# Last rows of four wide output products by token halves, with their norms and the next stage's first tiles, and squares added on VectorE

## The reference

```
for i in (0, 1):
    x  = x  + 0.5 * g1 * swiglu(modulate(rms(x),  sh1, sc1), pre_wi[i], pre_wo[i])    # D_FF = 2816
    xc = xc + 0.5 * g1c * swiglu(modulate(rms(xc), ...), pre_wi[i], pre_wo[i])
    o, oc = mixer(modulate(rms(x), sh2, sc2), modulate(rms(xc), ...))   # i=0 differential, i=1 window attention
    x = x + g2 * o ;  xc = xc + cg2 * oc            # xc only for i=0
    x = ffn_step(x, ..., post_wi[i], post_wo[i]) ;  xc likewise only for i=0
rms(x) = x * rsqrt(mean(x*x, over the 1024) + 1e-6)
modulate(h, shift, scale) = h * (1 + scale) + shift
```

## Time and profile before

| | |
|---|---|
| Median of 3 runs | 3052.09 us (3051.44 to 3053.5) |
| Span of the profiled execution | 3059.4 us |
| TensorE busy | 2886.5 us (94% of the span) |
| Weight loads busy | 2378.0 us |
| VectorE busy | 1669.1 us (55%) |
| ScalarE busy | 1225.2 us (40%) |
| GpSimd busy | 251.8 us (8%) |
| Mean granted clock of TensorE | 0.972 of full speed |
| Chain that ended last | PE 85%, DVE 9%, ACT 2%, DMA 2%, issue 1% |

### The profile page before, as it was taken

One profiled execution on the slowest core, in us unless ns is written; L12 is line 12 of the kernel. 1 busy time (PEld: TensorE's weight loads), 2 busy tenths in 40 slices (PEclk: granted clock), 3 DMA queues, 4 the chain that ended last, 5 costly groups with the idle time before them and its releaser, 6 DMA issues.

```text
span 3059.4 us, 46813 instructions
## 1 busy us (share of the span) xinstructions
PE 2886.5 (94%) x16044; PEld 2378.0 (78%) x16044; DVE 1669.1 (55%) x2800; ACT 1225.2 (40%) x1979; POOL 251.8 (8%) x163
## 2 busy tenths in 40 slices
PE   7999989997899999999988889998799899999999
PEld 4777866753678887788866379996799899888888
DVE  3333337756433333433337555577579777677765
ACT  4322223345232222322223544456445455455554
POOL 2000003200010000100003000000048200000000
PEclk9999999999899999999999989999999999999999
DMA  6444221262152222222231535552256555567754
GB/s 263 170 166 168 99 90 65 80 220 104 35 186 96 96 100 93 85 98 97 98 103 62 181 130 192 186 192 90 104 186 206 168 177 172 190 242 241 242 202 144
DMA packets 144831, 444.88 MB, mean 145 GB/s; under 512 B 16088, under 2 KB 44888, under 8 KB 144224
## 3 DMA queue, kind: packets, MB, share of 16 engines
q1 hardware_dynamic: 112896, 409.51, 38.9%
q10 hardware_dynamic: 31840, 34.13, 3.2%
HBM read 428.37 MB, written 15.20 MB: 145 GB/s over the span
## 4 chain that ended last, share of the span: by engine, by line
PE 85%; DVE 9%; ACT 2%; DMA 2%; issue 1%; SPq 1%; POOL 0%; ACTq 0%; DVEq 0%
PE bank L1565 21%; PE bank L1566 20%; PE bank L1567 20%; PE bank L1979 11%; PE bank L1581 2%; PE bank L1951 2%; PE bank L1804 1%; PE bank L1845 1%; DMA raw<-w_stream_dram 1%; PE bank L1588 1%; DVE cand L1364 1%; PE bank L1816 1%; DVE stage_rs L1037 1%; PE bank L1658 1%; PE bank L1836 1%
## 5 line engine op out<-in xcount | busy, mean ns | idle before, releaser
L1565 PE MATMUL bank<-H,w_hi 128*128 128x256 f32 (+1 forms) x3232 | 1097.4, 340 | 54.8 <-DVE H L1028 47.1
L995 DVE TENSOR_TENSOR w_lo<-raw,w_hi 128x1024 fp32r<-128x1024 f32 x584 | 714.7, 1225 | 700.9 <-ACT w_hi L568 696.0
L1566 PE MATMUL bank<-H,w_hi 128*128 128x256 f32 (+1 forms) x3232 | 1068.6, 331 | 0.0
L1567 PE MATMUL bank<-H,w_lo 128*128 128x256 f32 (+1 forms) x3232 | 1068.4, 331 | 0.0
L568 ACT ACTIVATE w_hi<-raw 128x1024 fp32r<-128x1024 f32 x628 | 660.0, 1052 | 250.9 <-PE bank L1567 208.3
L1565 PEld LDWEIGHTS bank<-H,w_hi 128*128 128x128 f32 x3232 | 623.8, 193 | 147.7 <-issue 83.0
L1566 PEld LDWEIGHTS bank<-H,w_hi 128*128 128x128 f32 x3232 | 624.2, 193 | 59.0 <-issue 5.6
L1567 PEld LDWEIGHTS bank<-H,w_lo 128*128 128x128 f32 x3232 | 623.0, 193 | 55.0
L1565 PE MATMUL bank<-act_hi,w_hi 128*128 128x512 f32 (+1 forms) x704 | 263.8, 375 | 0.0
L1567 PE MATMUL bank<-act_hi,w_lo 128*128 128x512 f32 (+1 forms) x704 | 255.5, 363 | 0.0
L1566 PE MATMUL bank<-act_lo,w_hi 128*128 128x512 f32 (+1 forms) x704 | 255.5, 363 | 0.0
(11 more groups left out here) (220 smaller groups left out, 2770.9 us busy)
## 6 DMA issues: line engine op xcount, KB each, us to landing
raw<-w_stream_dram SPq DMA_DIRECT2D x704, 512.0 KB, 3.3
ada_side<-w_stream_dram SPq DMA_DIRECT2D x52, 512.0 KB, 3.9
gelu_scratch<-gelu ACTq DMA_DIRECT2D x108, 128.0 KB, 3.5
gelu_in<-gelu_scratch ACTq DMA_DIRECT2D x108, 128.0 KB, 3.4
ada_start<-w_stream_dram SPq DMA_DIRECT2D x16, 512.0 KB, 13.7
bias<-bias_in_dram ACTq DMA_DIRECT2D x1, 3072.0 KB
X<-x_in_dram SPq DMA_DIRECT2D x1, 2048.0 KB, 10.5
mem<-mem_in_dram SPq DMA_DIRECT2D x1, 1024.0 KB, 17.0
```

What stands on the lines that cost most here:

```text
L995: nc.vector.tensor_tensor(w_lo[:, s, :], raw[:, s, :], w_hi[:, s, :].bitcast(F32), ALU.subtract).then_inc(lo_ready, 1)
L1565: nc.tensor.matmul(to, w_hi[:, s, cut], hi, start=first, stop=False, skip_group_check=True)
L1566: nc.tensor.matmul(to, w_hi[:, s, cut], lo, start=False, stop=False, skip_group_check=True)
L1567: return nc.tensor.matmul(to, w_lo[:, s, cut], hi, start=False, stop=last, skip_group_check=True)
```

## The change

`UPDATES` names the seven output products (`wo0`, `out_a`, `wo1`, `wo2`, `out_b`, `wo3`, `out_c`) with their halves and the number of late rows: ("LC", 1), ("LC", 2), ("LC", 1), ("LC", 1), and three times ("L", 0).

1. Late rows. In the four wide products the last row (in `out_a` the last two) is made for the L tokens and then for the C tokens, each half in a bank of its own. `half_done` tells VectorE that an L half is ready. A tile of a late row is free only after its C half.
2. Norm by halves. The norms behind them (`norm_by_halves`) run 16 steps of 256 tokens: eight chunks of L, eight of C. The L sums are closed inside the C half of the first late row (after 4 of its blocks), the C sums after the second step of the next stage's first tiles (`first_by_halves`). The updates, squares and sums of the C half and the splits of the last tiles (`next_splits`) are placed among the first steps of the L half.
3. Squares. TensorE no longer sums every row. VectorE adds the squares of rows 1 to 6 (1 to 5 in `out_a`) onto those of row 0 (`add_squares`, counted by `acc_ready`); TensorE sums that, then those of the last row or rows, at the end only (`x_sums`). The opening product of zeros is gone. This holds for all seven output products.
4. The Sqrt table is loaded before the rows of the output product (`root_table`) instead of after them, in the four FFNs and `out_b`.
5. The loops over rows are written out.

```diff
...
+UPDATES = (("LC", 1), ("LC", 2), ("LC", 1), ("LC", 1), ("L", 0), ("L", 0), ("L", 0))
...
+        def next_splits(stage, u, m):
+
+            per = WO_T if stage[:2] == "wo" else 1
+            tiles = [RING[stage] + per * m + k + AHEAD for k in range(per)]
+            if not late(u) or m < KC - 1:
+                return tiles, []
+            now = 1 if per > 1 else 0
+            return tiles[:now], tiles[now:]
...
```

On ScalarE:

```diff
+            def norm_by_halves(name, split_next, between):
...
+                rows = list(range(KC - late(u), KC))
+                root("L")
+                for t in split_next[:-1]:
+                    split(t)
+                high(0)
+                split(split_next[-1])
+                high(1)
+                for m in rows:
+                    squares(u, m, "C")
+                between()
+                high(2)
+                high(3)
+                root("C")
+                for step in range(4, 2 * KC):
+                    high(step)
...
+            def squares(update, m, halves):
...
+                act.wait_ge(x_done, piece_count(update, m, halves[0]))
+                if m >= 3:
+                    act.wait_ge(acc_ready, acc_count(update, min(m - 2, added_rows(update)[-1])))
...
+            def rows_out(update, m, tiles):
...
+                for t in split_now:
+                    split(t)
+                squares(update, m, halves if m < KC - n else "L")
...
```

On VectorE:

```diff
+            def norm_by_halves(name, split_next, rest_of_update):
...
+                turn_rs(0)
+                z(0)
+                for t in split_next[:-1]:
+                    split(t)
+                z(1)
+                low(0)
+                split(split_next[-1])
+                z(2)
+                low(1)
+                rest_of_update()
+                z(3)
+                low(2)
+                z(4)
+                low(3)
+                z(5)
+                low(4)
+                turn_rs(1)
+                for step in range(6, 2 * KC):
+                    z(step)
+                    low(step - 1)
+                low(2 * KC - 1)
...
+            def rows_out(stage, u, gate, per):
...
+                for m in range(KC):
+                    for t in next_splits(stage, u, m)[0]:
+                        split(t)
+                    if m - 1 in added_rows(u):
+                        add_squares(u, m - 1)
+                    if m < KC - n:
+                        dve.wait_ge(tile_used, RING[stage] + per * (m + 1))
...
```

On TensorE:

```diff
+            def x_sums(update, half):
...
+                pe.wait_ge(acc_ready, acc_count(update, added_rows(update)[-1]))
+                nc.tensor.matmul(sums_bank(half)[:, cut], ones, stage_sq[:, 0, cut], start=True, stop=False,
+                                 skip_group_check=True)
+                for m in direct:
+                    pe.wait_ge(x_sq_ready, piece_count(update, m, half[0]))
...
+            def first_by_halves(name, targets, t0):
...
+                for step in range(2 * KC):
+                    half, k = step // KC, step % KC
+                    pe.wait_ge(hl_ready, n["chunk_at"] + step + 1)
+                    for at, to in enumerate(targets):
+                        if step == 0:
+                            pe.wait_ge(lo_ready, split_at(t0 + at) + 1)
...
+                    if step == 1:
+                        x_sums(n["update"], "C")
...
+            def rows(update, row):
...
+                for half in "LC" if n else ():
+                    for m in range(KC - n, KC):
+                        pe.wait_ge(x_done, piece_count(update, m - 4 if half == "L" else 4 + m - (KC - n)))
+                        row(m, half, 3 if half == "C" and m == KC - n else None)
+                if not n:
+                    x_sums(update, halves)
...
```

More of the change, by code:

```diff
@@ L675, in ffn @@
                 wi_steps(act, f, chunks)
[L676 to L680, removed]
+                root_table()
+                for m in range(KC):
+                    rows_out(update, m, next_splits(f"wo{f}", update, m))
             def project(stage):
@@ L786, in project_out @@
             def project_out(stage, halves, update):
[L787 to L790, removed]
+                if stage == "out_b":
+                    root_table()
+                for m in range(KC):
+                    rows_out(update, m, next_splits(stage, update, m))
             act.wait_ge(in_loaded, 32)
@@ L828, in _ @@
             project_out("out_a", "LC", 1)
-            norm("post0")
+            norm_by_halves("post0", next_splits("out_a", 1, KC - 1)[1], nothing)
             ffn(1, "LC", 2)
-            norm("pre1")
+            norm_by_halves("pre1", next_splits("wo1", 2, KC - 1)[1], nothing)
             ffn(2, "LC", 3)
[L833 to L836, removed]
+            norm_by_halves("mix_b", next_splits("wo2", 3, KC - 1)[1], load_rope_mask)
             project("qkv_b")
@@ L1099, in ffn @@
                     dve.wait_ge(mod_ready, 5)
[L1100 to L1109, removed]
+                rows_out(f"wo{f}", up, lambda m, half: mod_col(layer, which, m, half), WO_T)
             def project(stage):
@@ L1253, in attend, with project_out @@
                     split(t)
[L1255 to L1264, removed]
+            def project_out(stage, gate, halves, up):
+                rows_out(stage, up, lambda m, half: sm("one") if gate is None else mod_col(gate, 5, m, half), 1)
             nc.vector.memset(zeros[:, :], 0.0)
@@ L1306, in _ @@
             norm("pre0", {1: first_half, 3: second_half})
-            ffn(0, 0, 2, "LC")
-            norm("mix_a")
+            ffn(0, 0, 2, "LC", 0)
+            norm_by_halves("mix_a", next_splits("wo0", 0, KC - 1)[1],
+                           lambda: late_rows("wo0", 0, "C", lambda m, half: mod_col(0, 2, m, half), WO_T))
             dve.wait_ge(table_loaded, 32)
@@ L1340, in _ @@
             norm("og_c")
-            project_out("out_c", None, "L")
+            project_out("out_c", None, "L", 6)
             norm("ffn_c")
@@ L1734, in ffn, with row @@
-                close_x_sums(update, halves)
+                def row(m, half, sums_at=None):
+                    cut = half_cols(half)
+                    whole_row = m < KC - late(update)
+                    to = bank[4 + m % 4] if whole_row else late_bank(update, m, half)
+                    for kk in range(WO_T):
+                        t = t1 + WO_T * m + kk
+                        pe.wait_ge(lo_ready, split_at(t) + 1)
+                        pe.wait_ge(act_lo_ready, FC * f + min(FC, KC * (kk + 1)))
+                        for k in range(min(KC, FC - KC * kk)):
+                            j = KC * kk + k
+                            ins = passes(to[:, cut], t % R, k, act_hi[:, j, cut], act_lo[:, j, cut], j == 0, j == FC - 1)
+                            if j == sums_at:
+                                x_sums(update, "L")
+                        if whole_row or half == "C":
+                            ins.then_inc(tile_used, 1)
+                    if not whole_row and half == "L":
+                        ins.then_inc(half_done, 1)
@@ new lines, in ffn @@
+                rows(update, row)
+            def rows(update, row):
+                halves, n = UPDATES[update]
+                for m in range(KC - n):
+                    if m >= 4:
+                        pe.wait_ge(x_done, piece_count(update, m - 4))
+                    row(m, halves)
+                for half in "LC" if n else ():
[4 more added lines that the diff above has]
+                    x_sums(update, halves)
```

228 lines of the change are left out of this document (159 added, 69 removed).

## The result

The changed kernel takes 2999.9 us (median of 4 runs, 2998.4 to 3005.9), the kernel before 3051.8 beside it: ratio 0.9825, interval 0.981 to 0.984, 52 us less. Forecast were 3010 us and a range of 2999 to 3028. The sign and the places were right, the size was 10 us short, and scaled to the 3052.1 us that the forecast starts from the result is 2998.7, just under the range.

What follows compares the result with a forecast made beforehand. It took TensorE, busy 94% of the span, as the bound. Terms -12.9, -12.8, -11.5, -4.3, -3.6, +0.7 and +1.9 sum to -42.5 us; from 3052.1 that gives 3009.6, stated as 3010, range 2999 to 3028.

Steps and rivals of the forecast that it cites:

- First tiles after the wide norm: At FFN outputs, late rows, halved norm and fewer sums save 12.9 us in mix_a, 11.5 in pre1, 12.8 in mix_b.
- The new chain: Behind FFN outputs: L norm done under the C half, three tiles end 28.5 us after the L half's end.
- The sums: Sums of squares taken out of rows save 0.86 us each wide, 5.2 us per wide FFN output.
- The additions in narrow stages: In out_b and out_c, six VectorE additions of 0.35 us each lie on the update path: +1.9 us per stage.
- `out_a` and `post0`: Attention output and its norm: H complete earlier, less a bare side-tile wait and a low clock, -4.3 us.
- The stall of 4 us: In out_a, TensorE waits some 4 us before the L sums because the L updates come late.
- bare wait for the side tiles: In post0, TensorE idles some 4 us because SyncE fetches ada_side only when all of H is written.
- the low clock behind it: In post0 after the side-tile wait, a lower clock loses 1.7 us, bounds 0 and 3.4.
- `post1`, `wo3`: wo3 saves 3.6 us, 3.1 from sums and 0.5 from the table; out_b's early Sqrt table saves 0.7.
- halved steps did not starve TensorE: Rival, chance 0.2: halved norm steps on three queues take 1.3 us, 14 us come back, 3024 us.
- The clock did not fall in the transitions: Rival, chance 0.1: short waits keep the clock low in the transitions, +8 us, 3018 us.
- The written-out code: Rival, chance 0.04: fetching some 3,000 more TensorE instructions stops TensorE inside rows; at 60 us the time is 3064.

Runs made afterwards that it cites:

- the ladder: Versions from the kernel before towards the changed one: loops written out 3049.4 us, then Sqrt table early 3045.9, then squares added on VectorE with whole last rows 3027.3.
- loops and table: Kernel before with loops over rows written out and the Sqrt table loaded ahead of the rows in the FFNs and out_b: 3045.9 us, ratio 0.9967.
- whole rows: Changed kernel without late rows, with the wide norm of whole rows behind them; squares on VectorE, loops and early table kept: 3027.3 us, ratio 0.9909.
- three: Changed kernel with side tiles of ffn(1) fetched early, additions behind the update, and the fourth tile's high split ahead of the Silu table: 2993.8 us.
- side_early: The early side fetch: changed kernel with ffn(1)'s side tiles in a buffer of their own, fetched before post0: 3000.9 us, ratio 0.9821.
- silu_later: Changed kernel with the high split of an FFN's fourth tile ahead of the Silu table load, ffn(1) to ffn(3): 3005.9 us, ratio 0.9841.

## Why the prediction was right in kind, and too small

The places and the new chains came as forecast, and the clock in the transitions too; the gain was 52 to 54 us and not 42.5. Two steps of the prediction failed most. It took 17.8 us for the first three tiles behind a wide norm in the kernel before, which measure 18.9, 3.3 us in three transitions; and it put the stretch from attention A to `out_a` at nothing, where 4.0 us went. Smaller misses in size make up the rest. Measured stage differences are the mean of the table's two profiles.

- **First tiles after the wide norm, mis-sized.** `mix_a` -14.3 against -12.9, `pre1` -13.7 against -11.5, `mix_b` -13.6 against -12.8. The step that failed is "After `wo0` it takes 12.4+5.4+12.4 = 30.2 us from the last product to the end of the first three tiles". Three tiles are 72 products; the windows I took hold 13 and 56. In the kernel before the 72 take 18.9 us, not 17.8:

```profile
455.30:474.20 18.90, 18.90 (x72) 15.26 (x72) 9.91 (x13) 7.49 (x14) 12.02 (x13) 0.86 0.09 28
...
1226.65:1245.55 18.90, 18.87 (x72) 15.42 (x73) 9.96 (x13) 9.06 (x15) 12.07 (x13) 0.85 0.08 28
```

  That is 1.1 us in each, 3.3 in all. The length is not the products' alone: with the loops written out the same 72 take 17.9 us in `pre1`, since less of them runs at the lower clock. The new chain itself was right: from the end of the L half to the end of the three tiles 28.5 us were forecast and 28.5 to 28.7 measured in `pre1`. The first product of the fourth tile starts 37.4 us after the start of the last row, where 38.2 were forecast.
- **The sums.** Right in kind, a little low: an update of a `wo` row follows the last after 14.96 us, before after 15.87, so 0.91 a sum against 0.86, 0.3 a stage.
- **The additions in narrow stages, mis-sized.** +1.9 forecast, +1.1 measured in each. The addition costs 0.34, as priced; I had kept the loop's 3.15 beneath it, and written out the chain is 3.06. Moved behind the update it costs nothing, so it was a link of the chain and no more.
- **`out_a` and `post0`.** -5.5 against -4.3. TensorE reached the L sums 24.7 us after the first update, not 22.9, for two of the three first tiles still had products to run. The stall of 4 us was 0.3. The path went over VectorE's updates anyway, and H was complete 1.3 us earlier than forecast. The bare wait for the side tiles (4 forecast, 5.3 and 4.2 measured) and the low clock behind it were right, and the early fetch shows their price: 5.8 to 6.7 us in this stage.
- **`post1`, `wo3`.** 5.0 us between `out_b`'s last update and attention C; 4.3 forecast (3.6 and 0.7 for the table). That this is close is partly luck: on the ladder loops and table bring 2.8 and the squares 2.1, where the sum had 1.2 (`wo3`'s 0.5 and `out_b`'s 0.7, for the table) and 3.1. Rows without a sum are 0.42 shorter, so the five sums alone make the 2.1; of the opening product, 0.86 in the sum, nothing shows here.
- **Left out.** Attention A to `out_a`, 4.0 us less though nothing is changed in it. The stages above sum to -49.9 where the forecast has -42.0 (its -42.5 with `out_b`'s opening product, 0.5, left out: it stands before the first update, in a stretch that differs by 5.3 between two profiles of the kernel before). With these 4.0 it is 53.9; medians and ratio say 52 to 54.

The rivals: halved steps did not starve TensorE. GpSimd's chunks took 0.55 to 0.92 us (the first 1.72) and started every 1.04 us in the mean, and TensorE's last eight steps are 1.08 us long; most of the first seven are longer (up to 2.55), with the sums and the waits in them. The clock did not fall in the transitions but for `post0`, as counted. The written-out code cost nothing that the ladder shows.

**What stays open.** Of 18 profiles, all five of the kernel before and its loop versions have 161 to 162 us from attention A to `out_a`, all five with additions moved everywhere 160 to 161, all six others with halves 157 to 158, and whole rows once each. It leans on the kernel and is not fixed by it; what tips it was not found. The clock alone is not it: the changed kernel and `three` both have a mean granted clock of 0.91 there and TensorE busy for 135.2 and 135.3 us, and take 157.0 and 160.1. Nor was why the medians of `side_early` and `silu_later` lie above what their stages gain.

## What to carry to other kernels

Halving the last row and the norm pays as far as the second half's products cover the first half's chain (with one late row instead of two in `out_a`, H was complete 2.5 us later), and only up to the next wait that the old gap had hidden: look for fetches tied to the end of that norm, and free their buffer first. Where a row is a chain over several engines, put side work behind the instruction that the next engine waits for: that was worth 2.0 us in `out_b` and in `out_c`, and about 1 at most in the wide `out_a`. When a stretch is timed by windows, count its products (tiles times 24) before the length is trusted, and compare its granted clock with that of a second version.

## What the runs showed of the hardware

A hardware loop over registers lengthened each step of a chain over VectorE and ScalarE by 0.1 us (3.15 against 3.05). The length of a stretch at half clock is not settled by the code: the same kernel passed the same stage in 157.1 and 160.4 us. The Trainium skill ("TensorE: Matmul & The Clock Gate", section "What's actually happening") says that the number of slow matmuls varies between runs of one kernel; the windows of whole rows agree. It puts the cost of the ramp under 1% of a typical span. This kernel falls to the lower level many times, and a mean granted clock of 0.98 (0.972 before) means up to 2% of its span, by an estimate from that mean. The 3.3 us between two profiles of whole rows are half of what the early side fetch is worth. In the transitions of the changed kernel gaps of about 1 us left the granted clock at 1.00; the one of 5.3 us was followed by about 3 us at 0.50.
